# First mixer: half of four output blocks' matmuls placed among the sparse attention's steps, which use six PSUM banks

## What is computed

```python
y_a = dsa_attention(q_a, k_a, v_a, q_idx, k_idx, w_idx, w_uv_a[l], top_k)      # sparse, 8 heads of 64
y_b = stick_breaking_attention(q_b, k_b, v_b)                                   # 8 heads of 64
merged = jax.nn.sigmoid(gate_a) * (y_a @ w_o_a[l]) + jax.nn.sigmoid(gate_b) * (y_b @ w_o_b[l])
x = x + merged @ w_out[l]
```

## Time and profile before

| | us |
|---|---|
| three runs | 2064.51, 2065.46, 2071.32 |
| median | 2065.46 |
| the profiled execution | 2064.34 |
| its span, first to last instruction | 2062.2 |
| PE, DVE, ACT busy in it | 1910.8, 957.2, 684.2 |
| mean granted clock of PE | 0.977 of full |

### The profile page before, as it was taken

One profiled execution on the slowest core, in us unless ns is written; L12 is line 12 of the kernel. 1 busy time (PEld: TensorE's weight loads), 2 busy tenths in 40 slices (PEclk: granted clock), 3 DMA queues, 4 the chain that ended last, 5 costly groups with the idle time before them and its releaser, 6 DMA issues.

```text
span 2062.2 us, 21538 instructions
## 1 busy us (share of the span) xinstructions
PE 1910.8 (93%) x8662; PEld 1371.4 (67%) x8662; DVE 957.2 (46%) x1521; ACT 684.2 (33%) x1115; POOL 87.7 (4%) x121
## 2 busy tenths in 40 slices
PE   8999999998999989999999999999999977888887
PEld 6888888765877767888888888876785333333332
DVE  5433544367656786544344447666772111111113
ACT  5322322345545354433222234655641101010110
POOL 0000000100000001000000000000001111111100
PEclk9999999998989999999999999999999999999999
DMA  6433332343333403333333323222189999999997
GB/s 198 143 97 108 96 93 82 72 74 59 67 56 63 103 26 126 99 92 97 88 102 102 92 83 103 70 57 57 31 298 400 405 406 410 406 410 412 411 413 304
DMA packets 262154, 351.21 MB, mean 170 GB/s; under 512 B 11872, under 2 KB 225888, under 8 KB 237472
## 3 DMA queue, kind: packets, MB, share of 16 engines
q1 hardware_dynamic: 252432, 326.42, 47.2%
q0 software_dynamic: 9616, 23.34, 3.2%
HBM read 337.19 MB, written 20.45 MB: 173 GB/s over the span
## 4 chain that ended last, share of the span: by engine, by line
PE 67%; DMA 17%; DVE 9%; ACT 4%; issue 1%; SPq 1%; DVEq 0%; POOLq 0%; ACTq 0%
PE bank L183 66%; DMA large<-w_up 14%; SPq L225 1%; DMA stage<-w_in 1%; PE bank L186 1%; ACT p L189 1%; ACT wH L189 1%; DMA large<-pair_results 1%; DVE y L195 1%; DVE PTL L195 1%; DVE p L198 1%; DVE score L201 0%; DVE st L207 0%; DMA xg<-token_rows,tok 0%; DVE cv L201 0%
## 5 line engine op out<-in xcount | busy, mean ns | idle before, releaser
L183 PE MATMUL bank<-hH,wH 128*128 128x512 f32 x1104 | 441.9, 400 | 16.3 <-DVE stage0L L195 10.0
L183 PE MATMUL bank<-hL,wH 128*128 128x512 f32 x1104 | 435.1, 394 | 0.0
L183 PE MATMUL bank<-large,xF 128*64 128x512 f32 x1024 | 243.5, 618 | 73.9 <-DMA large<-w_up 62.8
L189 ACT ACTIVATE wH<-stage 128x1024 fp32r<-128x1024 f32 (+3 forms) x231 | 227.6, 995 | 108.3 <-PE bank L183 83.6
L183 PEld LDWEIGHTS bank<-hH,wH 128*128 128x128 f32 x1104 | 211.3, 191 | 63.9 <-DVE stage0L L195 10.0
L183 PEld LDWEIGHTS bank<-hL,wH 128*128 128x128 f32 x1104 | 210.9, 191 | 45.0 <-issue 1.9
L183 PEld LDWEIGHTS bank<-large,xF 128*64 128x64 f32 x1024 | 82.3, 141 | 210.1 <-issue 154.9
L183 PE MATMUL bank<-hidH,wH 128*128 128x512 f32 x352 | 138.4, 393 | 2.0 <-DVE stage3L L195 0.8
L183 PE MATMUL bank<-hidL,wH 128*128 128x512 f32 x352 | 137.2, 390 | 0.0
L183 PE MATMUL bank<-large,hF 128*64 128x512 f32 x512 | 118.5, 605 | 2.2 <-DVE hF L195 2.2
L195 DVE TENSOR_TENSOR xF<-bank,gain 128x512 f32<-128x512 f32 x30 | 20.8, 692 | 156.8 <-PE bank L186 156.8
(11 more groups left out here) (493 smaller groups left out, 3263.9 us busy)
## 6 DMA issues: line engine op xcount, KB each, us to landing
large<-w_gate SPq DMA_DIRECT2D x64, 1024.0 KB, 29.2
large<-w_up SPq DMA_DIRECT2D x64, 1024.0 KB, 28.3
large<-w_down SPq DMA_DIRECT2D x64, 1024.0 KB, 29.2
stage<-w_in SPq DMA_DIRECT2D x58, 512.0 KB, 4.3
stage<-w_gate SPq DMA_DIRECT2D x44, 512.0 KB, 3.9
stage<-w_up SPq DMA_DIRECT2D x44, 512.0 KB, 3.8
stage<-w_down SPq DMA_DIRECT2D x16, 512.0 KB, 4.2
pair_results<-zero POOLq DMA_DIRECT2D x8, 512.0 KB, 2.9
```

Source lines behind the costliest of these rows:

```text
L183: return self.e.matmul(*a, **k) if self.e is not None else Nothing()
L189: return self.e.activation(*a, **k) if self.e is not None else Nothing()
```

## The change

Four blocks of 12 matmuls, the `ob` part of output blocks 0 to 3, leave the merge and become steps of their own, `out_b(m)`: 0 before `expand(0)`, 1 before `values(1)`, 2 before and 3 behind `expand(7)`. Blocks 0 and 1 write into banks 6 and 7 and keep them until DVE has used them in the merge. Therefore the takes of the sparse attention (and of the last four gate projections) name their bank, from a cycle over banks 0 to 5; blocks 2 and 3 and the `oa` of merge steps 0 to 3 take theirs from the same cycle. A weight unit is now freed by `oa` for the first four blocks. ACT and DVE prepare unit m + `ahead` at `out_b(m)`, at most up to unit 3, so units 2 and 3 are prepared at `out_b(0)` and `out_b(1)`; the merge steps 0 to 3 prepare up to unit m + 3, the later ones up to m + 2 as before. The part of the second DVE and ACT hunks that reads alike is left out.

```diff
--- before.py
+++ after.py
@@ -580,20 +580,31 @@
             def logits(p):
                 s = Step("logits", n=2 * p, i=jobs[2 * p][0])
                 s.heads = [4 * g + hh for _, g, hh in jobs[2 * p:2 * p + 2]]
-                s.banks = [banks.take(("pexp", n)) for n in (2 * p, 2 * p + 1)]
+                s.banks = [banks.take(("pexp", n), next(six)) for n in (2 * p, 2 * p + 1)]
                 s.p = probs[p] = [pr.take(("mm", "turn_p", n)) for n in (2 * p, 2 * p + 1)]
                 add(s)
 
             def turn_p(p):
                 i, _, hh = jobs[2 * p]
-                add(Step("turn_p", n=2 * p, i=i, k=hh, banks=[banks.take(("pt", n)) for n in (2 * p, 2 * p + 1)], p=probs[p]))
+                add(Step("turn_p", n=2 * p, i=i, k=hh, banks=[banks.take(("pt", n), next(six)) for n in (2 * p, 2 * p + 1)], p=probs[p]))
 
             def values(grp):
-                add(Step("values", n=grp, i=jobs[4 * grp][0], bank=banks.take(("ol", grp))))
+                add(Step("values", n=grp, i=jobs[4 * grp][0], bank=banks.take(("ol", grp), next(six))))
 
             def expand(grp):
                 i, g, _ = jobs[4 * grp]
-                add(Step("expand", n=grp, i=i, g=g, banks=[banks.take(("ya", grp, c2, 1)) for c2 in range(2)]))
+                add(Step("expand", n=grp, i=i, g=g, banks=[banks.take(("ya", grp, c2, 1), next(six)) for c2 in range(2)]))
+
+            six, outs = itertools.cycle(range(6)), {}
+
+            def out_weights(m):
+                return unit([(0, wcols("w_o_a", m * 128, 128, 0, 4)), (512, wcols("w_o_b", m * 128, 128, 0, 4))], 8, 128, ("mm", "ob" if m >= 4 else "oa", m))
+
+            def out_b(m, n):
+                s = Step("out_b", m=m, unit=out_weights(m), bank=banks.take(("gb", m), n))
+                outs[m] = s.unit, s.bank
+                s.unit.ahead = min(AHEAD, 3 - m)
+                add(s)
 
             vw_rows(0)
             project_ki()
@@ -793,26 +804,28 @@
             logits(0)
             logits(1)
             topk(1)
-            gate()
+            gate(next(six))
             turn_p(0)
             logits(2)
-            gate()
+            gate(next(six))
             evict()
             topk(1)
             turn_p(1)
             topk(2)
             logits(3)
-            gate()
+            gate(next(six))
             turn_p(2)
             logits(4)
             evict()
             values(0)
             topk(2)
+            out_b(0, 6)
             expand(0)
             topk(1)
             turn_p(3)
             logits(5)
             turn_p(4)
+            out_b(1, 7)
             values(1)
             logits(6)
             turn_p(5)
@@ -847,7 +860,9 @@
             expand(5)
             expand(6)
             values(7)
+            out_b(2, next(six))
             expand(7)
+            out_b(3, next(six))
 
 
 
@@ -864,8 +879,14 @@
             for n in range(4):
                 load_gate(n)
             for m in range(8):
-                s = Step("merge", m=m, u=unit([(0, wcols("w_o_a", m * 128, 128, 0, 4)), (512, wcols("w_o_b", m * 128, 128, 0, 4))], 8, 128, ("mm", "ob", m)))
-                s.ba, s.bb = banks.take(("ga", m)), banks.take(("gb", m))
+                s = Step("merge", m=m)
+                if m in outs:
+                    s.u, s.bb = outs[m]
+                    s.ba = banks.take(("ga", m), next(b for b in six if b not in (outs[2][1].at, outs[3][1].at)))
+                    banks.turn = 5
+                else:
+                    s.u = out_weights(m)
+                    s.ba, s.bb = banks.take(("ga", m)), banks.take(("gb", m))
                 s.s1, s.s2, s.mt = loaded[2 * m], loaded[2 * m + 1], mt.take(("mg", m))
                 add(s)
                 if m < 6:
@@ -1653,15 +1674,23 @@
                             t = mm3(s.bank.t[:, 128 * j:512], both(M.vb, slice(None), j, slice(c * 128, (c + 1) * 128)),
                                     both(M.SP[n % 2], slice(None), slice(o, o + N)), j == 0, j == 3)
                         t.then_inc(*did("mm", "b3", n))
+                    elif s.kind == "out_b":
+                        pe.wait_ge(*after("w_lo", s.unit.i))
+                        pe.wait_ge(*after("yb", 7))
+                        free(s.bank)
+                        for k in range(4):
+                            t = mm3(s.bank.t[:, :], (s.unit.H[:, 4 + k, :], s.unit.L[:, 4 + k, :]), (M.yb[0][:, k, :], M.yb[1][:, k, :]), k == 0, k == 3)
+                        t.then_inc(*did("mm", "ob", m))
                     elif s.kind == "merge":
                         pe.wait_ge(*after("w_lo", s.u.i))
                         if m == 0:
                             pe.wait_ge(*after("ya", 7, 1, 1))
-                            pe.wait_ge(*after("yb", 7))
                         free(s.ba)
                         for k in range(4):
                             t = mm3(s.ba.t[:, :], (s.u.H[:, k, :], s.u.L[:, k, :]), (M.ya[0][:, k, :], M.ya[1][:, k, :]), k == 0, k == 3)
                         t.then_inc(*did("mm", "oa", m))
+                        if m < 4:
+                            continue
                         free(s.bb)
                         for k in range(4):
                             t = mm3(s.bb.t[:, :], (s.u.H[:, 4 + k, :], s.u.L[:, 4 + k, :]), (M.yb[0][:, k, :], M.yb[1][:, k, :]), k == 0, k == 3)
@@ -2044,7 +2073,7 @@
                     elif s.kind == "dense_pair":
                         for g in s.pair:
                             weights_for(g.unit)
-                    elif s.kind in ("dense", "rows"):
+                    elif s.kind in ("dense", "rows", "out_b"):
                         weights_for(s.unit)
                     elif s.kind == "chunk_copy":
                         chunk_copy(s.c)
@@ -2146,7 +2175,7 @@
                         act.wait_ge(*after("mm", "b3", n))
                         act.activation(M.yb[0][pp, c, :], s.bank.t[pp, :], ACT.Copy).then_inc(*did("ybh", n))
                     elif s.kind == "merge":
-                        weights_for(s.u)
+                        weights_to(s.u.i + (3 if m < 4 else AHEAD))
                         table("sigmoid")
                         act.wait_ge(*after("sg%d" % s.s1.at, 2 * m))
                         act.activation(s.s1.t[:, :], s.s1.t[:, :], ACT.Sigmoid).then_inc(*did("sga", m))
...
```

## The result

| | median us | runs | ratio to before, 95% interval |
|---|---|---|---|
| before, beside it | 2069.4 | 20 | |
| the change | 2073.06 (2070.72 to 2077.61) | 20 | 1.0018 [1.0011, 1.0025] |
| before, in a second comparison | 2066.53 | 35 | |
| the change, in a second comparison | 2072.39 | 12 | 1.0028 [1.0019, 1.0037] |

The change costs 3.7 to 5.8 us where a gain of 3.5 was forecast. It stays within 0.3%, but 2073.06 lies above the range, which ended at 2068.5. Of the 11 us between 2062.0 and 2073.06, 3.9 are the base (the median of before was taken as 2065.46, and is 2069.4 over 20 runs) and 7.1 are the change.

The account below looks back on a forecast made before the run. DVE was taken to bound the sparse attention, PE the merge. Terms -11.1 + 2.7 + 0.4 + 2.7 + 1.8 = -3.5 us gave a median of 2062.0 us from 2065.46; range 2056.5 to 2068.5.

Parts of the forecast that it names:

- Taken out of the merge, -11.1: Merge: four blocks of 2.77 us leave it, saving 11.1 us if PE still bounds that stage.
- Put in at the end, +2.7: Around `expand(7)`: blocks 2 and 3 overfill PE holes of 1.41 and 1.40 us, costing 2.7 us.
- Put in at the start, +0.4: Before `expand(0)` and `values(1)`: block 0 fits its hole; block 1's excess and other short bank waits cost 0.4 us together.
- The sign that the prediction named for bank waits at more places: Sparse attention: DVE's idle time growing by more than 3 us would show the forecast wrong.
- Two splits, +2.7: Sparse attention: preparing weight units 2 and 3 there adds two subtractions and one wait to DVE's chain, 2.7 us.
- Six banks, +1.8: At `values(5)`: rotating over six banks makes PE wait for a later exponential, delaying DVE's `PTL` of `turn_p(12)` by 1.8 us.
- The rival "the clock falls on the path": `values(5)` to `values(7)`, or `out_b(2)`: a block at half clock takes up to 2.8 us more; 2064.8 us, chance 0.15.
- the local sum: Sparse attention through merge: the terms for removed blocks, inserted blocks, splits and bank waits add up to -3.5 us.
- "All later stages only shift": Everything behind the merge: claimed to move in time only, with no term added for it.
- The slow rival, the wait repeating at six groups: Sparse attention: the 1.8 us bank wait recurs at six other `values` groups, sum +7.3, 2072.8 us, chance 0.06.
- The base: Whole kernel before: median taken as 2065.46 us from three runs, uncertain by 2 or so.

Follow-up runs that it names:

- r1_after: The changed kernel run once more without an edit, compared with the kernel before: median 2072.39 us, ratio 1.0028.
- r2_before_shifted: The kernel before with only the turn of the bank rotation shifted by 4 ahead of the second SwiGLU: ratio 1.0018 to before.
- r2_seven_late: Against the kernel before: three blocks moved (one before `expand(0)`, two around `expand(7)`), seven banks, unit 2 split only at the tail, old turn kept: ratio 0.9982.
- r3_seven_again: The same kernel as r2_seven_late, measured once more against the kernel before: ratio 0.9984.

## Why the prediction was wrong

- **Taken out of the merge, -11.1:** right. PE doesn't wait in it, and from its first matmul to the first on `mg` it takes 33.4 us, not 44.4 (-11.0).
- **Put in at the end, +2.7:** right. From `values(7)` to the merge 9.14 us against 6.84: +2.3.
- **Put in at the start, +0.4:** too small. The bank wait at the first turn is 0.5 us by itself, and with the clock low `out_b(1)` took 4.44 us, not 2.77, and made DVE wait 1.58 us. The sign that the prediction named for bank waits at more places, over 3 us of new idle time of DVE, came up (5.2 us), and was for the larger part not theirs: 2.2 us are bank waits (0.51 and 1.70), 1.6 the wait at `out_b(1)`, 0.5 the one at the second split.
- **Two splits, +2.7:** right; 2.9 us by themselves [0.8, 5.0].
- **Six banks, +1.8:** the place, the wait (1.51 us) and DVE's idle time (1.70 us) are those of the forecast. Alone they cost 2.9 us [0.8, 5.2].
- **The rival "the clock falls on the path":** it happened, and was mis-sized. It had one block of 2.77 us at half rate, up to 2.8 us, and a chance of 0.15. Three stretches lay on the path, and the local sum is missed by 2.7 and 4.9 us in the two profiles. By the starts of DVE's reductions into `st`, the three cost 1.6, 0.3 and 0.4 us in the first; in r1_after two of them cost 1.6 and 1.4, and the one at the tail 1.5. What else speaks for it: the same instructions take 2.3 us more or less by the place of these stretches alone, and two other placements gain what their sums say, to within about 1 us. What it takes to remove it was not found.
- **"All later stages only shift":** the step that failed outright. The change hands the later stages other banks, PE gets a wait of 2.3 us 600 us behind the edit, and the line `banks.turn = 5` stood in the diff. With the clock's 3 to 5 this takes the sum from -3.5 to +1.8 to +3.8. What is left of the measured 3.7 to 5.8 stands as low clock inside mixer 2, in two places. With the shift a stretch of 3.4 us fell 166 to 176 us behind its start in four of five profiles (where it was the only one and the wait was 2.3, mixer 2 was 1.6 us longer than 291.0), without it in one of nine. And one fell at 196 to 201 us in all four profiles of kernels with four moved blocks, in none of the ten others; without the shift mixer 2 took 291.0 and 290.8 us with it, some 2.2 more than the 288.6 to 289.0 of the profiles with neither. The wait and the two, 2.3 + 1.6 + 2.2, are the 6.1 us by which mixer 2 of the change's first profile is longer than before's. Why the clock falls at these places is open: r2_before_shifted had the wait and no low clock in mixer 2.
- **The slow rival, the wait repeating at six groups:** it did not happen, though its time, 2072.8, was nearest. The Trainium skill, "Perfetto Trace Analysis", section "Matmul Optimizations", asks for all 8 banks; its direction holds here (six banks alone cost 0.14%), but by two waits, 0.5 and 1.8 us, and not at many steps; three blocks over seven banks gained as much as two blocks over eight.
- **The base:** three runs gave 2065.46, and later sets of 20 to 35 runs of before medians of 2066.5 to 2069.4. The "ahead" column shows a source of the spread: 300.6 to 302.5 or 306.4 to 306.8 us for the same instructions. The range had 2 us for this.

## What to carry to other kernels

When takes from a ring of buffers get names, find out what the ring's turn is behind the edit, and compare the buffer numbers of every later stage; an order printed without them looks unchanged. A hole that PE loses may have been the one behind which its clock was low at no cost: ask where the low stretch goes next, and price each term on PE's path at the low clock too. A change of a few parts of a thousand needs a base of more than three runs.

## What was not expected of the hardware

The low stretches, 3.4 us and longer, lie at places that differ between executions of one program. Ahead of the sparse attention the same kernel had 44 us of them in one profile and 58 in another (r2_seven_late, r3_seven_again), and took 300.6 and 306.7 us; over all 14 profiles it is 44 to 55 us where this part took up to 302.5, and 58 to 65 where it took 306.4 or more. Over a whole profile they add up to 82 us (r2_seven_late, the fastest, 2058.30) to 126 us (r2_before_shifted, 2073.71). PE was busy throughout in each of the three of the change's first profile; what it did before the first of them was to wait 2.57 us.
